# Seven instead of five query blocks shared by two chunks of tokens, with eight instead of nine slots for experts' rows

## What is computed

```
for l in range(DEPTH):                                   # 2
    h = rmsnorm(x, norm_mix_g[l]);  proj = h @ w_in[l]
    y = concat(conv(proj), attention(proj), ssm(proj))   # each normed
    x = x + y @ w_out[l]
    x = x + memory_cross_attention(rmsnorm(x), rmsnorm(mem), w_mq[l], w_mkv[l], w_mo[l])
    x = x + peer_ffn(rmsnorm(x), peer_wq[l], keys[l], peer_u[l], peer_v[l])
# peer_ffn, for 128 tokens xc at a time:
    q = (xc @ w_q).reshape(128, 8, 2, 128)               # w_q: 1024 x 2048
    sc = einsum('chid,hikd->chik', q, sub_keys)          # top 16 + top 16 -> best 16 experts
    act = gelu(einsum('chkd,cd->chk', u_tab[expert], xc))
    out = einsum('chk,chkd->cd', gate * act, v_tab[expert])
```

## Time and profile before

| | us |
|---|---|
| median of 3 runs | 1686.9 (1686.73 to 1688.77) |
| the profiled execution | 1689.31 |
| its span, first to last instruction | 1687.3 |
| PE busy | 1540.3 (91%) |
| DVE busy | 1162.5 (69%) |
| ACT busy | 744.8 (44%) |
| POOL busy | 584.0 (35%) |
| moved by DMA | 674.08 MB, 399 GB/s over the span |

### The profile page before, as it was taken

One profiled execution on the slowest core, in us unless ns is written; L12 is line 12 of the kernel. 1 busy time (PEld: TensorE's weight loads), 2 busy tenths in 40 slices (PEclk: granted clock), 3 DMA queues, 4 the chain that ended last, 5 costly groups with the idle time before them and its releaser, 6 DMA issues.

```text
span 1687.3 us, 19145 instructions
## 1 busy us (share of the span) xinstructions
PE 1540.3 (91%) x6354; PEld 896.4 (53%) x6354; DVE 1162.5 (69%) x2896; ACT 744.8 (44%) x2025; POOL 584.0 (35%) x527
## 2 busy tenths in 40 slices
PE   9999899899999999988999889988999999777776
PEld 8757675457567656434645446434656554232232
DVE  7821899865877658986555667995556667666655
ACT  4142444764465333484433353465444434333333
POOL 0000444433334333353333343242333544343331
PEclk9999999999999999999999999999999999999999
DMA  9638999999999999999999999999999999999997
GB/s 383 261 125 326 359 422 420 421 421 420 420 419 420 419 420 421 420 416 421 421 421 420 420 413 421 402 417 398 421 411 419 421 421 421 421 421 422 420 422 291
DMA packets 93859, 674.08 MB, mean 399 GB/s; under 512 B 10408, under 2 KB 10688, under 8 KB 12480
## 3 DMA queue, kind: packets, MB, share of 16 engines
q0 software_dynamic: 73728, 536.90, 76.9%
q1 hardware_dynamic: 19888, 135.69, 19.8%
q10 hardware_dynamic: 144, 0.26, 0.0%
HBM read 671.76 MB, written 1.05 MB: 399 GB/s over the span
## 4 chain that ended last, share of the span: by engine, by line
PE 42%; DMA 29%; DVE 8%; ACT 5%; issue 2%; POOL 0%; ACTq 0%; POOLq 0%
DMA slots<-expert_rows,expert 29%; PE bank L1013 23%; PE bank L483 8%; DVE slots L2055 4%; PE bank L686 4%; PE bank L980 2%; PE bank L996 2%; ACT diag L1537 1%; DVE sg L1586 1%; ACT coef L1559 1%; ACT L1554 1%; PE bank L773 1%; PE bank L751 1%; ACT gel L1554 0%; DVE products L1804 0%
## 5 line engine op out<-in xcount | busy, mean ns | idle before, releaser
L1013 PE MATMUL bank<-slots,diag 128*128 128x512 f32 x1914 | 904.0, 608 | 123.9 <-ACT diag L1537 120.3
L1157 POOL DMA_INDIRECT slots<-expert_rows,expert x512 | 582.1, 1137 | 1079.2 <-PE bank L1013 867.6
L2055 DVE CUSTOM_DVE_ANT_0 slots<-slots,htok 128x1024 f32<-128x1024 f32 x512 | 625.7, 1223 | 380.3 <-DMA slots<-expert_rows,expert 379.4
L1013 PEld LDWEIGHTS bank<-slots,diag 128*128 128x128 f32 x1914 | 347.9, 193 | 538.6 <-issue 327.0
L1554 ACT ACTIVATE gel<-dot 128x2 f32<-128x2 f32 (+1 forms) x258 | 52.5, 203 | 609.8 <-DVE dot L2055 609.3
L483 PEld LDWEIGHTS bank<-hT,ring 128*128 128x128 f32 x1408 | 171.2, 193 | 39.9 <-issue 38.5
L483 PE MATMUL bank<-hT,ring 128*128 128x128 f32 x1408 | 172.1, 276 | 1.0 <-ACT hT L1193 1.0
L1537 ACT ACTIVATE diag<-ident,coef 128x128 f32<-128x128 f32 x479 | 168.1, 394 | 8.4
L1559 ACT ACTIVATE coef<-gel,gexp 128x1 f32<-128x1 f32 x512 | 123.0, 287 | 10.4
L1554 ACT ACT_TABLE_LOAD x69 | 88.5, 1283 | 1.2
L1586 DVE SCALAR_TENSOR_TENSOR sg<-pad,prm,sg 128x128 f32<-128x128 f32 x240 | 71.6, 343 | 0.0
(11 more groups left out here) (374 smaller groups left out, 1500.4 us busy)
## 6 DMA issues: line engine op xcount, KB each, us to landing
ring<-w_blocks SPq DMA_DIRECT2D x88, 1024.0 KB, 9.2
slots<-w_blocks SPq DMA_DIRECT2D x23, 1024.0 KB, 13.3
slots<-expert_rows,expert POOLq DMA_INDIRECT x512, 15.9
kept<-w_blocks SPq DMA_DIRECT2D x4, 1024.0 KB, 14.9
keys<-w_blocks SPq DMA_DIRECT2D x2, 1024.0 KB, 10.6
phasor<-w_blocks SPq DMA_DIRECT2D x2, 1024.0 KB, 9.9
kv<-w_blocks SPq DMA_DIRECT2D x2, 1024.0 KB, 13.8
prm<-small SPq DMA_DIRECT2D x2, 768.0 KB, 12.7
```

Source lines behind the costliest of these rows:

```text
L1013: last = mm(bank[h][:, :], diag[:, i % DIAGS, :], slots[:, SLOT[n], D + h * 512:D + (h + 1) * 512], start=m == 0, stop=n == end - (ph == N ...
L1157: nc.gpsimd.indirect_dma_start(slots[:, s, :], None, (experts0_d, experts1_d)[n // PER // NC], bass.IndirectOffsetOnAxis(ap=idx[q % 2][:, ...
L2055: v.tensor_tensor_reduce(out=slots[:, s, 0:D], in0=slots[:, s, 0:D], in1=htok[:, ph % 2, :], scale=1.0, scalar=0.0, op0=ALU.mult, op1=ALU.add,
```

## The change

Seven blocks are shared in each layer, heads 1 to 7. A third kept room is added, and the kept rooms hold heads 1, 2 and 3; it takes the memory of the ninth slot, so eight slots remain. Head 4 becomes a late head in layer 1 also and goes into `T`, head 5 into a new room, the matrices of `prm` with the tiles `uT` and `va` laid behind them, and head 6 stays in `kv`. With that (constants are put on one line here): the early places are nine instead of ten, only one block of pass 1 is held in a slot, the block in `T` waits for the last rotated products of the SSM instead of for its outputs, the one in the matrices' room for the squares of the SSM's outputs. The matrices of layer 1 are loaded only when head 5 of pass 1 has been read, ahead of pass 2's first memory block; DVE's wait for them stands before its first use of them, and its setup of layer 1 ends some ticks later. The load of the memory rows for layer 1 stands two blocks earlier in SP's order.

```
-EARLY = 32, WIDE = 10, AHEAD = 1, STAY = 2, SLOTS = 9
+EARLY = 30, WIDE = 9,  AHEAD = 0, STAY = 3, SLOTS = 8
-HEADS = [[0, 1, 2, 3], [5, 0, 7, 6, 1, 4, 2, 3], [0, 1, 2, 3, 4], [7, 0, 1, 2, 6, 5, 3, 4]]
-KEPT = [[3, 4], [3, 4]];  POCKETS = [[6, 5], [6, 5]]
+HEADS = [[0, 1, 2, 3], [4, 0, 5, 7, 6, 1, 2, 3], [0, 1, 2, 3], [7, 0, 1, 2, 6, 5, 3, 4]]
+KEPT = [[1, 2, 3], [1, 2, 3]];  POCKETS = [[6, 4, 5], [6, 4, 5]]
-HELD = {2: 8, 3: 7}
-SLOT = [n % 7 for n in range(20)] + [(6, 8, 0, 1, 7, 2, 3, 4, 5)[n % 9] for n in range(NG - 20)]
+HELD = {2: 7}
+SLOT = [n % 7 for n in range(20)] + [(6, 0, 7, 1, 2, 3, 4, 5)[n % 8] for n in range(NG - 20)]
...
-        prm = sb("prm", [P, NPRM])
+        prm = sb("prm", [P, NPRM + 2 * CT * P])
-        uT = sb("uT", [P, CT, P])
-        va = sb("va", [P, CT, P])
+        uT = prm[:, NPRM:NPRM + CT * P].rearrange("p (t s) -> p t s", t=CT)
+        va = prm[:, NPRM + CT * P:].rearrange("p (t s) -> p t s", t=CT)
...
-            return T[:, :, :, :].rearrange("p t r s -> p (t r s)")[:, 0:KT * BW]
+            if p == POCKET + 1:
+                return T[:, :, :, :].rearrange("p t r s -> p (t r s)")[:, 0:KT * BW]
+            return prm[:, NVEC:NVEC + KT * BW]
...
-                    nc.sync.dma_start(prm[:, NVEC:], prm_d[1, :, NVEC:]).then_inc(mats_in, 16)
-                if n == FIRST["wq"] + 2 and stage == 1:
+                if (l, n) == (1, FIRST["mk"]):
+                    full(("wq", POCKETS[0][2], 1))
+                    nc.sync.dma_start(prm[:, NVEC:NPRM], prm_d[1, :, NVEC:]).then_inc(mats_in, 16)
+                if n == FIRST["wq"] and stage == 1:
                     full(("mo", 1, 1))
                     nc.sync.dma_start(memX[1][:, :, :], ...)
...
                 if p == POCKET + 1:
-                    full(("ssm y", NC * l + 1))
+                    eng.wait_ge(turned, 2 * 4 * (NC * l + 2))
+                if p == POCKET + 2:
+                    eng.wait_ge(ssm_squared, CT * (NC * l + 2))
```

More of the change, by code:

```diff
@@ L56 @@
 RING = 3
[L58 to L63, removed]
+EARLY = 30
+WIDE = 9
+AHEAD = 0
+STAY = 3
 POCKET = WIDE + STAY + 2
-SLOTS = 9
+SLOTS = 8
 DIAGS = 4
@@ L100 @@
 SSM_LATER = [6, 0, 0, 0]
-HEADS = [[0, 1, 2, 3], [5, 0, 7, 6, 1, 4, 2, 3], [0, 1, 2, 3, 4], [7, 0, 1, 2, 6, 5, 3, 4]]
-KEPT = [[3, 4], [3, 4]]
-POCKETS = [[6, 5], [6, 5]]
+HEADS = [[0, 1, 2, 3], [4, 0, 5, 7, 6, 1, 2, 3], [0, 1, 2, 3], [7, 0, 1, 2, 6, 5, 3, 4]]
+KEPT = [[1, 2, 3], [1, 2, 3]]
+POCKETS = [[6, 4, 5], [6, 4, 5]]
 WQ_AT = [[89, 91, 93, 95], [94 + i * 5 // 2 for i in range(8)],
-         [94 + 4 * i for i in range(5)], [94, 98] + [106 + 8 * i for i in range(6)]]
+         [94 + 4 * i for i in range(4)], [94, 98] + [106 + 8 * i for i in range(6)]]
 def late_heads(ci):
@@ L310, in build @@
         rows_in = sem("rows_in")
-        loaded = [sem(f"loaded{s}") for s in range(POCKET + 2)]
+        loaded = [sem(f"loaded{s}") for s in range(POCKET + 3)]
         arrived = [sem(f"arrived{s}") for s in range(SLOTS)]
@@ L1047, in _ @@
                     first = FIRST["mq"] if p == POCKET else FIRST["out"] + 3
-                    behind = max(k for k in range(j) if order[k] == (l, first))
+                    behind = next(k for k in range(len(order)) if order[k] == (l, first) and second[k])
                     issue.insert(issue.index(behind), j)
@@ L1074, in _ @@
                     nc.sync.dma_start(gains[:, :], rows_d[0, :, :]).then_inc(rows_in, 16)
-                    nc.sync.dma_start(prm[:, NVEC:], prm_d[0, :, NVEC:]).then_inc(mats_in, 16)
+                    nc.sync.dma_start(prm[:, NVEC:NPRM], prm_d[0, :, NVEC:]).then_inc(mats_in, 16)
                 if j == 5:
@@ L1662, in setup_ops @@
                 eng.wait_ge(phasor_ready, 2 * (l + 1))
-                eng.wait_ge(mats_in, 16 * (l + 1))
                 co, si = T[:, :, 0, 1], T[:, :, 1, 1]
@@ L1681, in setup_ops @@
                 cf, cg = cfg[l]
+                eng.wait_ge(mats_in, 16 * (l + 1))
                 yield v.tensor_tensor(cf, Cl[:, :, :, :], fr.unsqueeze(2).unsqueeze(3).to_broadcast([P, ST, 2, 32]),
@@ L2153, in route_tick @@
     return G0 + TOP * (q - 1) - 6 + (n - 1)
-SETUP_TICK = [lambda n: 2 if n < 6 else 5 if n < 16 else 6 + n // 8 if n < 56 else 20, lambda n: 71 + n // 3 if n < 49 else 98 + (n - 49) // 3 if n < 56 else 102 + (n - 56) // 4]
+SETUP_TICK = [lambda n: 2 if n < 6 else 5 if n < 16 else 6 + n // 8 if n < 56 else 20, lambda n: 71 + n // 3 if n < 49 else 98 + (n - 49) // 3 if n < 56 else 102 + (n - 56) // 4 if n < 71 else 109 + (n - 71) // 2]
 ANGLE_OP = (51, 54)
```

## The result

The changed kernel takes 1691.97 us (median of 22 runs, 1689.02 to 1696.71); the kernel before took 1688.32 us in the same comparison (22 runs, 1686.73 to 1692.78). The ratio is 1.0023, with a 95% interval of 1.0017 to 1.0030: slower by 3.9 us (2.9 to 5.1), where 4.6 us less were forecast and 1682.3 us predicted. Of the difference of 9.7 us, 1.4 is that the three runs from which the prediction started had the low median of 1686.9; the rest, 8.3 to 8.5, is the change.

The account below looks back on a forecast made before the run. From 200 us on DMA at 421 GB/s was taken as the bound. Loads -4.98, slot +1.2, transposes -0.8 gave -4.6: profiled 1689.3 to 1684.7 us, less 2.4 for timed runs, 1682.3; range 1679.5 to 1690.0.

Parts of the forecast that it names:

- One slot less: Eight slots for expert rows: free in the last stretch, costing where the queue runs empty; +1.2 us, bounds 0 to +12.4.
- half a row at 1090: The slot's chosen price: half of a 2.49 us row at the DMA gap near 1090 us, +1.2 us.
- the ninth slot was the cover of bursts: Rival: queue empties a row earlier whenever PE or DVE holds slots; three places 1689.4 us, five 1694.4; chance 0.15.
- New SP waits: Loads waiting in SP's in-order queue in both layers; each priced at nothing, though lateness could cost up to +6 a layer.
- Some 25 us later: Head 5's load waits for the SSM's squares, estimated this much later, holding up two output blocks; priced at nothing.
- The layer 0 detour: Two loads more between 230 and 345 us, given back at 463 to 505; taken as 0, bounds 0 and +5.0.
- has by then moved the same bytes: Why layer 0's lag costs 0: behind 640 us DMA is the bound again and the bytes are equal.
- The loads: 118 blocks instead of 122; net two fewer after 165 us, in the third and fourth chunks: -4.98 us, or 0.
- only the third chunk's load pays: Rival: fourth chunk's loads leave inside continuous PE, eight slots may not hold the lead; -1.3, 1685.6 us; chance 0.20.
- Late transposes: Fourth chunk's token transposes (L927) move 16 ticks forward, halving a 1.7 us DMA loss: -0.8 us, bounds -1.7 and +3.1.
- only fill PE: Head 4's own matmuls and routing move into 1100 to 1150 us and merely fill PE there; no price given.
- a row's way: Sign: a row's time on its way in the last stretch falls from 15.2 us to near 12.7 with eight slots.

Follow-up runs that it names:

- l1: Kernel before with the change's layer 1 part only, nine slots for rows (one head's result left wrong): -2.7 us against the kernel before.
- a9: Changed kernel with nine slots for rows instead of eight, the third kept room given up (head 2 left wrong): 1688.68 us, -0.8 against the kernel before.
- b8l0: Kernel before with rows in eight slots to the end of layer 0 and nine from there: +3.0 us.
- b8: Kernel before with rows in eight of its nine slots throughout, nothing else changed: 1692.27 against 1688.86 us, +2.7.
- lean8: Kernel before with two fourth-chunk loads left out and rows in eight slots from row 200 on: -0.8 us.
- aord: Changed kernel with head 5's load, which waits for the squares, put behind the output blocks in SP's order: +0.7 us against the kernel before.
- mixo: Layer 0 as before, layer 1 as changed, eight slots from row 200, head 5's load behind the output blocks: -1.2 us against the kernel before.
- six: Kernel before with six shared heads in layer 1 instead of five, head 4 late, nine slots, 121 loads: 1687.43 us, -1.4.
- det: Kernel before with the change's layer 0 part only, nine slots (head 2 of the second chunk left wrong): +1.2 us.
- mix: Complete kernel: layer 0 as before with nine slots, layer 1 as changed, eight slots from row 200 on: +1.0 us against the kernel before.
- lean: Kernel before with two ring loads of the fourth chunk left out (heads 1 and 2 left wrong), nine slots: -2.4 us.
- b7: Kernel before with rows in seven of its nine slots throughout: 1702.6 us, +14.2.

## Why the prediction was wrong

From before to after in three runs: l1 -2.7, then layer 0 as after +1.9 (a9), then one slot less +4.7 (after): +3.9. The forecast for the same three steps was -5.8, 0 and +1.2. All three were wrong in the same direction.

- **One slot less, +1.2 forecast, +4.7 measured.** This is the step that failed first. The bounds (0 to 12.4) held it; the choice of half a row at 1090 did not. I took the price from the places where the trace of before showed DMA falling off. But those gaps show where nine slots are too few already; what the ninth covers shows nowhere, as DMA stands at 421 there. Without the other edits the largest part is paid in layer 0 (b8l0 +3.0), a stage that has no price in the prediction's sum and where the earlier trace rows show 421 GB/s; 216 to 240 us, where before has DVE busy for 23.46 of 24 us and PE for 22.28, is the likely place. That is the rival "the ninth slot was the cover of bursts", whose time for three places was 2.5 above before; it was given 0.15. The rule of the Trainium skill that the prediction weighed ("Perfetto Trace Analysis", section "Optimization Strategy": a repeated gap can mean too little room for the next tile) agrees in its direction, as one slot less cost 2.7 us and two 14.2. Its sign does not tell the two apart from one trace: the same gap stands at 361 GB/s with eight slots (b8) and at 368 in one trace with nine (lean8), and at 421 it is not there at all (before).
- **New SP waits, nothing each.** Wrong for one of the four: head 5's wait for the squares. "Some 25 us later" was near (32.8 us), and the two output blocks were not late for PE. What I left out is that a standing SP leaves the DMA queue to the rows alone, and rows stop where slots are held. With eight slots it costs 2 to 3 us (aord and mixo). How much of the 4.7 that is stays open: a9 stands as long and has the same gap, and only l1 against six speaks for the short row queue as the partner that makes it cost. The other three waits show nothing: PE's waits in 470:545 are none, in 0:171 they are 1.0 us for a block in a slot (0.5 before), and DVE's in 500:570 name no matrices.
- **The layer 0 detour, 0 forecast, about +1.4 (0.1 to 2.7).** A lag came (7 us in after, where 5.0 were worked out, though part of such a lag can come without the detour), and the argument that DMA "has by then moved the same bytes" failed in part: DVE waits longer for rows from 200 to 380 (21.4 us in after, 19.4 in det and 12.6 in a9 against 10.7), and behind it, from 380 to 640, DMA moves 413 GB/s in after, 416 in a9 and 417 in det against 420. Why it doesn't catch up there is not shown; that the slots are full is my reading.
- **The loads, -4.98 forecast.** The third chunk's load gave its 2.5, in every kernel that leaves it out (2.4 to 2.5 between rows 200 and 256 in after, a9, l1 and six; 2.0 in mix and mixo). The fourth chunk's gave about half, 1.2 each (lean), in a stretch where PE is full; that it is the slots which can't hold the lead is argued, not shown (lean8 is open). The rival "only the third chunk's load pays" was nearer than the forecast.
- **Late transposes, -0.8 forecast, some +1.1 (six, with 1.5 either way, so zero is not excluded).** The 3.07 us wait for a root did go, as L929 shows in PE's timeline of after, now at 1098.27 with no wait. But the gap moved rather than closed: with head 4's own matmuls, which I let "only fill PE", PE loses its pauses at 1110, and two later waits of PE for diagonals took 2.66 us (1.93 at the same place before) and 4.15:

```profile
1098.27 1.04 PE L929 MATMUL bank<-ident,htok 128*128 128x128 f32 x8
...
1108.01 2.43 PE L1015 MATMUL bank<-slots,diag 128*128 128x512 f32 x4 [2.66 <-ACT diag L1543]
...
1145.63 3.78 PE L1015 MATMUL bank<-slots,diag 128*128 128x512 f32 x4 [4.15 <-ACT diag L1543]
```

The parts add up to the sum: -2.5 - 1.2 + 1.1 is l1's -2.7, near enough. Of what was to show it, the bytes, some 2.5 us a row in the last stretch and the third chunk's end came as said; a row's way there was not measured. DMA's share nearly did (1.00 or 1.01, but for 0.98 from 1080 to 1180, as before, a stage that the prediction's rows leave out), while its rate fell to 416, 413 and 403: the share was the wrong sign. What stays open is how the 3.7 us that the slot costs in layer 1 (mix against l1) divide among late head 4, SP's order and the lead that saved loads give; only the order was tried by itself.

## What to carry to other kernels

What a buffer covers is not visible at the gaps of the kernel that has it: look instead for stretches in which the engines that free the buffers are full, and ask how long the queue lasts there. A byte saved is worth its time only where DMA sets the end and there is room for the lead; inside a stretch that hangs on PE it was worth about half. One trace of a kernel isn't enough to place a loss of a few microseconds: compare it with every trace that has the same code in that stretch. And a wait on an in-order queue has to be priced not just by who needs the transfer, but by what else then feeds DMA.

## What the runs showed of the hardware

In the last stretch, 1320 to 1660, the number of slots in use didn't change the rate: 421 GB/s with nine (before), eight (after) and seven (b7). DMA's share and its rate part company in the gaps: b8 shows a share of 0.96 beside 361 GB/s (0.86 of 421), and after the share 0.95 beside 370 in 228:236, so a share near 1 doesn't say that nothing is lost. And a pause of PE cost twice here: after PE's 4.15 us of idleness before 1145.63, the granted clock of 1145:1150 was 0.50, the lower level, and the four matmuls there took 3.78 us, where the same four take 1.88. The windows, both of after:

```profile
228.00:236.00 8.00, 7.26 (x42) 5.16 (x41) 7.91 (x26) 5.95 (x15) 5.03 (x5) 1.00 0.95 370
1145.00:1150.00 5.00, 4.37 (x5) 1.85 (x6) 2.46 (x5) 4.89 (x14) 0.31 (x1) 0.50 1.01 419
```
